# A fused decoder step on one core: latent-cache pages spread over their slots by quarters, scores and rope columns turned by VectorE, a group's softmax and weighing one page sooner

## What is computed

```python
def mla_keys(latent, w_uk, w_uv, k_norm_nope):
    c, kr = latent[..., :KV_LORA], latent[..., KV_LORA:]
    kn = rms_norm((c @ w_uk).reshape(bsz, s, MLA_HEADS, NOPE_DIM), k_norm_nope)
    v = (c @ w_uv).reshape(bsz, s, MLA_HEADS, V_DIM)

def mla_scores(qn, qr, kn, kr):
    s = einsum('bqhd,bkhd->bhqk', qn, kn) + einsum('bqhr,bkr->bhqk', qr, kr)
    return s * MLA_SCALE

def partial_softmax(s, v):
    m = max(s, axis=-1); p = exp(s - m[..., None])
    return m, sum(p, axis=-1), einsum('bhqk,bkhd->bhqd', p, v)
```

## Time and profile before

| | |
|---|---|
| median of the runs | 1484.63 us |
| the profiled execution's own time | 1484.91 us |
| its span, first to last instruction | 1483.1 us |
| busy: PE / DVE / ACT / POOL | 99% / 55% / 59% / 15% |
| chain that ended last: PE / DVE / ACT | 97% / 2% / 1% |
| mean granted PE clock | 0.998 of full |
| mean busy share of the DMA engines in the page loop | 0.41 |
| ACT copies of the scores (L857) and of the rope columns (L852) | 18.6 us and 11.7 us in all |

### The profile page before, as it was taken

One profiled execution on the slowest core, in us unless ns is written; L12 is line 12 of the kernel. 1 busy time (PEld: TensorE's weight loads), 2 busy tenths in 40 slices (PEclk: granted clock), 3 DMA queues, 4 the chain that ended last, 5 costly groups with the idle time before them and its releaser, 6 DMA issues.

```text
span 1483.1 us, 26962 instructions
## 1 busy us (share of the span) xinstructions
PE 1473.2 (99%) x9284; PEld 1221.0 (82%) x9284; DVE 813.6 (55%) x1596; ACT 878.8 (59%) x2836; POOL 216.0 (15%) x111
## 2 busy tenths in 40 slices
PE   9999999999999999999999999999999999999998
PEld 7877777877877778778777777788777999999998
DVE  5864445555445563555554555645423766787643
ACT  5545678686566675576855666765766353444432
POOL 3001111211121111111221111111313000000000
PEclk9999999999999999999999999999999999999999
DMA  9542315643245443255323464322654465555551
GB/s 286 169 116 36 78 31 129 153 96 63 61 98 128 119 91 71 61 128 135 83 61 68 102 153 73 68 62 64 169 100 128 151 222 196 171 171 171 190 178 58
DMA packets 263714, 173.92 MB, mean 117 GB/s; under 512 B 165464, under 2 KB 212088, under 8 KB 263448
## 3 DMA queue, kind: packets, MB, share of 16 engines
q1 hardware_dynamic: 263266, 171.94, 44.5%
q10 hardware_dynamic: 318, 0.33, 0.1%
HBM read 132.63 MB, written 6.74 MB: 94 GB/s over the span
## 4 chain that ended last, share of the span: by engine, by line
PE 97%; DVE 2%; ACT 1%; issue 0%; POOL 0%; DVEq 0%; ACTq 0%
PE ps L1991 17%; PE ps L1993 16%; PE ps L1992 16%; PE ps L2400 6%; PE ps L2401 6%; PE ps L2402 5%; PE ps L2031 2%; PE ps L2012 2%; PE ps L2084 2%; PE ps L2348 2%; PE ps L2349 2%; PE ps L2085 2%; PE ps L2086 2%; PE ps L2350 2%; PE ps L1869 2%; PE ps L2150 2%
## 5 line engine op out<-in xcount | busy, mean ns | idle before, releaser
L846 ACT ACTIVATE ksq<-ps 128x128 f32<-128x128 f32 x1024 | 268.1, 276 | 295.0 <-PE ps L1993 293.7
L1991 PE MATMUL ps<-ukh,cTh 128*128 128x512 f32 x1024 | 417.9, 408 | 0.3 <-DVE cTl L1233 0.3
L1993 PE MATMUL ps<-ukh,cTl 128*128 128x512 f32 x1024 | 401.7, 392 | 0.0
L1992 PE MATMUL ps<-ukl,cTh 128*128 128x512 f32 x1024 | 400.4, 391 | 0.0
L700 POOL TENSOR_TENSOR rk<-kss,mhalf 128x32 f32<-128x32 f32 x32 | 179.7, 5616 | 496.8 <-DVE kss L1659 496.8
L1991 PEld LDWEIGHTS ps<-ukh,cTh 128*128 128x128 f32 x1024 | 192.8, 188 | 53.8 <-issue 17.1
L1993 PEld LDWEIGHTS ps<-ukh,cTl 128*128 128x128 f32 x1024 | 192.3, 188 | 42.6
L1992 PEld LDWEIGHTS ps<-ukl,cTh 128*128 128x128 f32 x1024 | 193.2, 189 | 34.1
L846 ACT ACTIVATION_READ_ACCUMULATOR ksq<-ps 128x1 f32 x1024 | 212.2, 207 | 0.0
L834 ACT ACTIVATE cTr<-turned 128x1024 uint16<-128x1024 uint16 x126 | 173.9, 1380 | 10.9 <-PE ps L2015 6.7
L1035 ACT ACTIVATE wh<-wraw 128x2048 fp32r<-128x2048 f32 x44 | 84.3, 1916 | 131.7 <-PE ps L2402 127.2
(11 more groups left out here) (501 smaller groups left out, 2692.4 us busy)
## 6 DMA issues: line engine op xcount, KB each, us to landing
clat<-cache_mla SPq DMA_DIRECT2D x128, 256.0 KB, 2.6
wraw<-w_in SPq DMA_DIRECT2D x16, 1024.0 KB, 5.1
wraw<-w_up SPq DMA_DIRECT2D x16, 1024.0 KB, 5.3
wraw<-w_down SPq DMA_DIRECT2D x16, 1024.0 KB, 5.0
braw<-w_in SPq DMA_DIRECT2D x24, 512.0 KB, 4.1
crope<-cache_mla SPq DMA_DIRECT2D x128, 32.0 KB, 2.4
sst<-state_gdn SPq DMA_DIRECT2D x32, 128.0 KB, 3.3
gdn_sample<-sst SPq DMA_DIRECT2D x32, 128.0 KB, 2.0
```

Source lines behind the costliest of these rows:

```text
L846: i = nc.scalar.activation(ksq[:, P * h:P * h + P], ps[:, k % 3, P * h:P * h + P], ACT.Square, accum_out=kss[:, n // 4 % 2, n % 4, 4 * hal ...
L1991: mm(out, cTh[:, n % 2, c], ukh[:, c, cols], start=c == 0, stop=False)
L1992: mm(out, cTh[:, n % 2, c], ukl[:, c, cols], start=False, stop=False)
L1993: i = mm(out, cTl[:, n % 2, c], ukh[:, c, cols], start=False, stop=c == 3)
```

## The change

- `page` writes a page's 128 rows as 32 partitions x 4 slots: page q = u % 4 of a group goes to partitions 32q to 32q + 31 of the group's four slots, row 32j + a to partition 32q + a of slot j. Each slot then holds a quarter of each of the four pages. One semaphore per group (`group_landed`, 8 DMAs x 16) takes the place of one per page.
- `query_products` runs 16 matmuls of 128 x 8 weights and 128 columns (chunk outside, quarter inside, accumulating over the chunks) and 8 matmuls of 32 x 8 weights and 128 columns for the rope part, four row groups on four column groups. The sum over the chunks is now made in PSUM. `rope_columns` and `score_columns` are gone, and ACT's `turned_rope` and `score_rows`.
- DVE turns the rope rows (`turned_rope`, t = 2) and the scores (`score_parts`, t = 0) with its own transpose in 32 x 32 blocks, 128 x 256 numbers each, the second from PSUM.
- `maxima` and `exps` move from t = 3 to t = 2, `weigh(g-1)` runs at t = 3 between the two halves (before: `weigh(g-2)` at t = 1), `probabilities` and `accumulate` from t = 1 to t = 0, SP's reload from i = 8m + 3 (`pv_used` >= m - 1, group m + 1) to i = 8m + 7 (`pv_used` >= m, group m + 2).
- In the front the rope query is placed by 16 small matmuls (`qro`, 128 x 32 weights, 32 columns) and two DVE copies; four copies, the two DMAs and POOL's clearing of qeff go.

```diff
-                sp.dma_start(clat[:, u, :], rows_[:, 0:LAT]).then_inc(S(f"page_landed{u}"), 16)
-                sp.dma_start(crope[:, u, :], rows_[:, LAT:LW]).then_inc(S(f"page_landed{u}"), 16)
+                q, slots = u % 4, slice(u - u % 4, u - u % 4 + 4)
+                sp.dma_start(clat[32 * q:32 * q + 32, slots, :], rows_[:, 0:LAT].rearrange("(j a) n -> a j n", a=32)).then_inc(S(f"group_landed{u // 4}"), 16)
+                sp.dma_start(crope[32 * q:32 * q + 32, slots, :], rows_[:, LAT:LW].rearrange("(j a) n -> a j n", a=32)).then_inc(S(f"group_landed{u // 4}"), 16)
...
-                n = (i - 3) // 2 + RING - 8
-                if i % 8 == 3 and i >= 16 and n < NT:
-                    sp.wait_ge(S("pv_used"), i // 8 - 1)
+                n = (i + 1) // 2 + RING - 8
+                if i % 8 == 7 and i >= 15 and n < NT:
+                    sp.wait_ge(S("pv_used"), i // 8)
...
-                if t == 2:
-                    turned_rope(g)
-                if t == 3:
-                    score_rows(g)
                 beside(2 * n)
                 squares(n, 0)
-                if t == 3 and g >= 1:
+                if t == 2 and g >= 1:
                     exps(g - 1)
...
-                v.wait_ge(S(f"page_landed{n % RING}"), 32 * (n // RING) + 32)
+                v.wait_ge(S(f"group_landed{n // 4 % 3}"), 128 * (n // RING) + 128)
...
+            def turned_rope(gg):
+
+                wait(v, "qk_done", gg)
+                u = 4 * (gg % 3)
+                V.transpose(rpT[:], crope[:, u:u + 4, :].rearrange("p j n -> p (j n)")).then_inc(S("rope_ready"), 1)
+
             def score_parts(gg):
-                v.wait_ge(S("st_done"), gg + 1)
-                V.tensor_reduce(sparts[:, gg % 2].rearrange("p t a h -> p t (a h)"), stp.rearrange("p t (c n) -> p t n c", c=4)[:, :, 0:16, :], AX, ALU.add).then_inc(S("s_parts"), 1)
+
+                v.wait_ge(S("qk_done"), gg + 1)
+                V.transpose(sparts[:, gg % 2].rearrange("p x j r -> p (x j r)"), ps[:, B_SCORE, 0:256]).then_inc(S("s_parts"), 1)
...
+                if t == 2:
+                    turned_rope(g)
                 if t == 0 and g >= 1:
                     score_parts(g - 1)
                 if t == 1 and g >= 1:
                     scaled(g - 1)
-                if t == 1 and g >= 2:
+                if t == 0 and g >= 2:
                     probabilities(g - 2)
                     accumulate(g - 2)
-                if t == 3 and g >= 1:
+                if t == 2 and g >= 1:
                     maxima(g - 1)
...
                 for c in range(4):
-                    mm(ps[32 * c:32 * c + 16, B_SCORE, :], qeff[:, s, c, :], cTr[:, c, :], start=True, stop=False)
-                for t in range(4):
-                    r = slice(64 * (t % 2), 64 * (t % 2) + 64)
-                    k = mm(ps[32 * t:32 * t + 16, B_SCORE, P * t:P * t + P], qeff[r, s, 4, :], rpT[r, P * (t // 2):P * (t // 2) + P], start=False, stop=True)
+                    for q in range(4):
+                        mm(ps[32 * q:32 * q + H, B_SCORE, 0:P], qeff[:, s, c, :], cTr[:, c, :].rearrange("p (j q a) -> p q j a", q=4, a=32)[:, q], start=c == 0, stop=c == 3)
+                for x in range(2):
+                    for q in range(4):
+                        r = slice(32 * q, 32 * q + 32)
+                        k = mm(ps[32 * q:32 * q + H, B_SCORE, P:2 * P], qro[r, s, x, :], rpT[r].rearrange("p (j x a) -> p x j a", x=2, a=32)[:, x], start=x == 0, stop=x == 1)
...
+                if i == 2:
+                    pe.wait_ge(S("qrs_ready"), 1)
+                    p_ = begin_a("qro")
+                    for x in range(4):
+                        for q in range(4):
+                            j = mm(p_[32 * q:32 * q + 32, 32 * x:32 * x + 32], consts[:, C_ID.start + 32 * x:C_ID.start + 32 * x + 32], qr[:, :, TP:T], start=True, stop=True)
+                    a_done(j)
...
-                if t == 0 and g >= 1:
-                    score_columns(g - 1)
-                if t == 1 and g >= 2:
-                    weigh(g - 2)
-                if t == 2:
-                    rope_columns(g)
                 beside(2 * n)
                 keys(n, 0)
                 if t == 2 and g >= 2 and g % 4 == 1:
                     latent_columns(g // 4 - 1)
-                if n == NT - 1:
-                    score_columns(g)
+                if t == 3 and 1 <= g < NG - 1:
+                    weigh(g - 1)
                 beside(2 * n + 1)
                 keys(n, 1)
```

More of the change, by code:

```diff
@@ L141 @@
 PAIR_B = ["cs", "rwA", "rwB", "vt", "kt", "ut1", "krow", "ut2", "urow", "ut3", "ut4", "ut5"]
-FRONT_A = ["ns", "rots", "qrow0", "qrow1", "rope0", "rope1", "qcol0", "qcol1", "rope2", "rope3", "rot0", "rot1", "rot2", "rot3", "snew"]
+FRONT_A = ["ns", "rots", "qrow0", "qrow1", "qro", "rope0", "rope1", "qcol0", "qcol1", "rope2", "rope3", "rot0", "rot1", "rot2", "rot3", "snew"]
 FRONT_A += [f"nope{h % 2 * H + h // 2}" for h in range(2 * H)]
@@ L221, in build @@
         rsq, o = place("rsq", [P, 3, T], F32, o)
-        qeff, e = place("qeff", [P, NS, 5, 16], F32, taken["rsq"][0])
+        qeff, e = place("qeff", [P, NS, 4, H], F32, taken["rsq"][0])
+        qro, e = place("qro", [P, NS, 2, H], F32, e)
         idr, e = place("idr", [P, P], F32R, e)
@@ L271, in build @@
         qk, o = place("qk", [P, 2, H, NS], F32, o)
-        qr64, o = place("qr64", [P, 4, NS], F32, o)
         assert o <= 212800, o
@@ L326, in build @@
         prows, o = place("prows", [P, 512], F32, o)
-        sparts, o = place("sparts", [P, 2, 4, 2, H], F32, o)
         lacc, o = place("lacc", [P, 512], F32, o)
@@ L456, in build @@
         trp = ps[:, B_TR, :].rearrange("p (c n) -> p c n", c=4)
-        stp = ps[:, B_SCORE, :].rearrange("p (t n) -> p t n", t=4)
+        sparts = prows[:].rearrange("p (y x j r) -> p y x j r", y=2, x=2, j=4)
         def sum_bank(gg):
@@ L577, in front_loads @@
             def front_loads(i):
[L578 to L581, removed]
                 if i == F_NOPE + 6:
@@ L695, in _ @@
             nc.gpsimd.memset(mhalf[:], -0.5).then_inc(S("pool_clear"), 1)
-            g.wait_ge(S("pool_clear"), 4)
+            g.wait_ge(S("pool_clear"), 3)
             def group(gg, y):
@@ L847, in squares @@
                 i.then_inc(S("ksq_ready"), 1)
[L849 to L857, removed]
             def exps(gg):
@@ L1242, in scaled @@
                 v.wait_ge(S("rk_ready"), gg + 1)
-                V.tensor_tensor(ssc[:, y], sparts[:, y, :, 0, :], rk[:, y], ALU.mult).then_inc(S("s_half"), 1)
+                V.tensor_tensor(ssc[:, y], sparts[:, y, 0, :, 0:H], rk[:, y], ALU.mult).then_inc(S("s_half"), 1)
                 v.wait_ge(S("s_half"), gg + 1)
-                V.tensor_tensor(ssc[:, y], sparts[:, y, :, 1, :], ssc[:, y], ALU.add).then_inc(S("s_ready"), 1)
+                V.tensor_tensor(ssc[:, y], sparts[:, y, 1, :, 0:H], ssc[:, y], ALU.add).then_inc(S("s_ready"), 1)
             def maxima(gg):
@@ L1317, in front_dve @@
                         V.tensor_copy(qrow[:, g], a_bank(f"qrow{g}")).then_inc(S("a_read"), 1)
+                    V.tensor_copy(qro[:].rearrange("p s l (a b) -> p b l a s", b=2)[:, 0], a_bank("qro")[:, 0:64].rearrange("p (l a s) -> p l a s", l=2, a=4))
+                    V.tensor_copy(qro[:].rearrange("p s l (a b) -> p b l a s", b=2)[:, 1], a_bank("qro")[:, 64:128].rearrange("p (l a s) -> p l a s", l=2, a=4)).then_inc(S("a_read"), 1)
                 if i in (3, 5):
@@ L1978, in transposes @@
             def transposes(n):
-                pe.wait_ge(S(f"page_landed{n}"), 32)
+                pe.wait_ge(S("group_landed0"), 128)
                 wait(pe, "ct_raw", n)
@@ L1994, in keys @@
                 i.then_inc(S("half_done"), 1)
-            def rope_columns(gg):
-                for u in range(4 * gg, 4 * gg + 4):
-                    pe.wait_ge(S(f"page_landed{u % RING}"), 32 * (u // RING) + 32)
-                wait(pe, "s_parts", gg)
-                for m in range(2):
-                    u = (4 * gg + 2 * m) % RING
-                    k = nc.tensor.transpose(ps[:, B_SCORE, P * m:P * m + P], crope[:, u:u + 2, :].rearrange("p u n -> p (u n)"), ident)
-                k.then_inc(S("rope_done"), 1)
             def query_products(gg):
@@ L2008, in query_products @@
                 pe.wait_ge(S("rope_ready"), gg + 1)
-                pe.wait_ge(S("qeff_ready"), 1)
+                pe.wait_ge(S("a_read"), a_count("qcol1"))
                 wait(pe, "s_parts", gg)
                 for c in range(4):
-                    mm(ps[32 * c:32 * c + 16, B_SCORE, :], qeff[:, s, c, :], cTr[:, c, :], start=True, stop=False)
-                for t in range(4):
-                    r = slice(64 * (t % 2), 64 * (t % 2) + 64)
-                    k = mm(ps[32 * t:32 * t + 16, B_SCORE, P * t:P * t + P], qeff[r, s, 4, :], rpT[r, P * (t // 2):P * (t // 2) + P], start=False, stop=True)
-                k.then_inc(S("qk_done"), 1)
-            def score_columns(gg):
```

(7 more changed lines are left out.)

13 lines of the change are left out of this document (2 added, 11 removed).

## The result

The changed kernel takes 1487.68 us (median of 20 runs, 1485.29 to 1490.13) against 1484.34 us (20 runs, 1483.35 to 1484.95): a ratio of 1.0025, 95% interval 1.0018 to 1.0031. It is slower by 3.3 us where 13 us of gain were forecast. Its runs also lie 4.8 us apart, those of before 1.6. Two single executions of all those in this document, 1683 and 2413 us, ran throughout at a lower mean granted clock (0.81 and 0.56) and are in no ratio.

What follows compares the result with a forecast made beforehand. TensorE's own instructions were taken to bound the page loop. Transposes -20.8, rope products +6.4 and front +1.1 us made -13.3 against 1484.9, so 1471.5 us was forecast, range 1467 to 1480.

Steps and rivals of the forecast that it cites:

- the score and rope transposes: PE, page loop: removing them saves 0.44 and 0.21 us a group, 20.8 us over 32 groups.
- the query products: PE, page loop: latent part unchanged, rope part 0.54 us, +0.20 us a group, 6.4 us in all.
- `qro`: Front, on PE: 16 small matmuls add 1.1 us once, between 0.2 and 3.2.
- Rivals 1 and 2: Query products: rope row groups in series, 1510, chance 0.06; small records issue-bound at 0.0425 us each, 1488, chance 0.05.
- What I cost at nothing, and its cover: List of DVE transposes, sooner `maxima`, fewer ACT copies and SP's reload, all priced at zero because slack covers them.
- Weighing keeps its four matmuls and their price and only changes place.: PE, page loop: moving the weighing was counted as no change in time.
- that leaves 1.8 us for 0.4: DVE's 0.4 us rope transpose has 1.8 us before PE begins the products at t = 3, so PE doesn't wait.
- and over 5 us in the others: Slack of the turn behind SP's page DMAs: 1.5 us in three bare groups, over 5 us in the other groups.
- none due in PE within 2 us: Work behind the sooner `maxima` in DVE's queue isn't needed by PE within 2 us, so its 0.4 us wait costs nothing.
- Rival 3: Page loop feed becomes late: turns 3 us later give 1476, DVE waiting for POOL in every group 1481; chance 0.1.
- signs under "right": Query products 1.5 to 1.7 us, 0.5 for rope; PE's loop waits under 3 us; loop 12 us shorter, later stages same.
- The last one under "wrong": Sign of a late feed: keys waiting for cTl or products for rpT, with planes waiting for landings or `mall` for POOL.

Runs made afterwards that it cites:

- e8: Kernel before with the moved softmax, weighing and sums alone, SyncE's reload left in its old slots 8m + 3: 1489.14 us, ratio 1.0031.
- e9: Kernel before with only `maxima` and `exps` moved to t = 2; weighing, sums and reload unmoved: 1484.33 us, ratio 1.0001.
- e1: Changed kernel with `z_low(3)` ahead of `maxima(31)`, and `weigh(31)` and `latent_columns(3)` each one z unit later: 1482.50 us, ratio 0.9992.
- e2: Changed kernel with VectorE's `turned_rope` one page sooner, at t = 1, nothing else: 1484.26 us, ratio 1.0005.
- e10: Changed kernel with only SyncE's reload split in two halves around `turn(4m + 6)`: 1485.49 us, ratio 1.0006.
- the three repairs: Changed kernel with the last group's new order, `turned_rope` at t = 1 and the reload split around the turn: 1479.45 us, ratio 0.9967.
- e4: Kernel before with the moved softmax, weighing, sums and reload alone; products, transposes and page layout as before: 1489.57 us, ratio 1.0036.
- e12_weigh_t0: e5 with `weigh(g - 2)` at t = 0, maxima and exponentials at t = 3, sums at t = 1, reload behind the turn: 1481.05 us, ratio 0.9978.
- e3: Changed kernel with softmax, weighing, sums and reload back at their places of before, new products and transposes kept: 1507.69 us, ratio 1.0163.
- e5: Changed kernel with both the last group's new order (e1) and `turned_rope` at t = 1 (e2): 1481.51 us, ratio 0.9979.
- e6: e5 with SyncE's reload in two halves, two pages before `turn(4m + 6)` and two behind it: 1479.45 us, ratio 0.9967.
- e11: Kernel before with the last group's new order, as in e1: 1484.06 us, ratio 0.9998.
- e7: e5 with VectorE's `probabilities` and `accumulate` back at t = 1, `maxima` staying at t = 2: 1481.76 us, ratio 0.9981.

## Why the prediction was wrong

**Right.** The price of each term: the score and rope transposes (0.43 and 0.22 us measured for 0.44 and 0.21), the query products (+0.22 for +0.20), 0.44 us for a transpose on VectorE (0.4). `qro` takes 0.5 us for the 1.1 I gave it. The sum of -13 us is the change's static worth. Rivals 1 and 2 fell: 16 rope records in four row groups that share one bank take 0.55 us, not 1.74, and the 32 latent records are 0.031 us apart, not 0.0425. The Trainium skill (TensorEngine Tiling (Array Packing), "Gotcha 1: PSUM Pressure") says that different row tiles can't access one bank at the same time; the trace doesn't agree, and it decides. Merge and MLP stayed the same, as said (267.2 us in both); the z units, which also stand behind the loop, didn't.

**Wrong: "What I cost at nothing, and its cover".** The 16.6 us between the forecast change (-13.3) and the measured one (+3.3) lie there and in the last group's chain, which the list doesn't have.

| given back | by | us |
|---|---|---|
| weighing no longer covers waits at t = 1 (on the kernel before, reload unmoved) | e8; nothing in e9 | 4.6 |
| last group: GpSimd's chain, VectorE's order, clock | e1 | 5.2 |
| rpT behind side work | e2 | 3.4 |
| turn held by the reload | e10 | 2.2 |

They come to 15.4, and -13.3 + 15.4 = +2.1 against +3.3 measured. Each holds to some 2 us and they aren't independent (one of the rpT waits came from a late turned page), so that the sum comes so near is in part luck: the three repairs together gave 8.2 us, not 10.8.

- *"Weighing keeps its four matmuls and their price and only changes place."* This step failed most, together with the last group. Its price is the same; its place was worth some 5 us (4.6 in e8, 5.4 in e4). I had read "nobody feeds PE late" as slack everywhere. It says only that the waits were filled.
- *"that leaves 1.8 us for 0.4"* was read in a group with nothing beside it, and for rpT that is the easy case. Groups 6 and 28, with a reciprocal chain at t = 2, had none.
- For the turn I had it that only the bare groups are tight, "and over 5 us in the others". The waits for the turned page, 29 of them in the loop, lie mostly outside the three bare groups, so the average page length says little there. How many of them reached PE the traces don't show one by one; e10 puts them at 2.2 us in all.
- *"none due in PE within 2 us"* for what stands behind `maxima` holds in the loop of the kernel before (e9; in the changed one it wasn't tried alone), and not for `maxima(31)`. The last group wasn't looked at, although a shorter loop moves PE against a chain that doesn't become shorter with it.
- Rival 3, *the feed becomes late*, named one of the four causes, the late turn, and its price of 1476 - 1471.5 = 4.5 us isn't far from the 2.2. The others aren't in it: `maxima` costs something only behind the loop, and the weighing's place and the reciprocal chain are no matter of the feed.

Of the signs under "right", those on the products appeared (1.63 us, 0.55 of them for the rope records), and those on PE's waits (10.8 us for under 3) and on the loop (2.4 us shorter for 12) didn't. The last one under "wrong" appeared: query products waiting for rpT, planes waiting for landings, `mall` for GpSimd.

## What to carry to other kernels

When the bounding engine hardly waits, ask of every piece that leaves its queue or changes place which wait it was filling: one run with the moved part alone on the old kernel tells it. Read slack where the other queues are fullest, not in the bare iteration, and follow the first and the last iteration by themselves, since a chain through another engine isn't made shorter with the loop (here it even grew by 5 us). If data is laid out so that a slot needs a whole group, the load has to come sooner (two pages here, one and a half in e12_weigh_t0), and all that frees the slots with it.

## What the runs showed of the hardware

- A wait of PE of some 2 us can cost as much again in clock. In e1_tail PE waited 2.12 us for `lrl` where the changed kernel waited 0.95, and the window below has a clock of 0.83: the half page with the wait is 1.2 us longer than in the changed kernel, the next one, without any wait, 1.6. In the kernel before no ten-microsecond window of the loop lies under 0.99. The length of one wait doesn't decide it: in e12_weigh_t0 a window of 0.83 follows a wait of 1.41 us, and in the changed kernel none follows one of 1.76 us.

```profile
650.00:660.00 10.00, 7.88 (x40) 6.73 (x40) 5.23 (x14) 5.92 (x21) 0.90 (x2) 0.83 0.30 59
```

- The kernels whose profiled run has such a window (after, e1, e2, e3, e5, e10, e12) have runs 4 to 7 us apart; before, e4, e6, e8, e9 and e11, with none, 1 to 2 us. e7 has none and 4.4 us. So that the clock makes the spread is argued, not shown.
- GpSimd in the tail of after: its `gate`, a sum of two numbers, took 2.29 us beside VectorE's 2.28 us subtraction, which began at 1146.25. In the kernel before VectorE began its own only at 1148.85, and `gate` took 0.18 us. The maximum over the partitions came 7.71 us after the end of `gate`, and before 5.92 us. All fourteen profiled runs fall into these two kinds: 0.18 us and then 5.9 to 6.2 (before, e3, e4, e8, e9, e11), or 2.3 us and then 7.7 to 7.9 (the other eight). The first kind has no wait of PE in the z units, e3 among them, which has the new products. Whether the long `gate` and the long gap have one cause, and what the tail would be without them, wasn't tried. First after, then before:

```profile
1146.29 2.29 POOL L697 TENSOR_TENSOR gate<-mhalf 1x1 f32<-1x1 f32 x1 [0.60 <-DVE ssc L1233]
1156.29 0.45 POOL L698 PARTITION_ALL_REDUCE smax<-ssc  x1 [7.71 <-issue]
```

```profile
1148.52 0.18 POOL L702 TENSOR_TENSOR gate<-mhalf 1x1 f32<-1x1 f32 x1 [0.60 <-DVE ssc L1245]
...
1154.63 0.45 POOL L703 PARTITION_ALL_REDUCE smax<-ssc  x1 [5.92 <-issue]
```
